# Reordering the start of the second layer of a two-layer diffusion block: weight splits, root and first norm tile interleaved, and one modulation block moved

## The reference

```python
for l in range(DEPTH):                       # DEPTH = 2
    mod = silu(c) @ ada_w[l] + ada_b[l]      # 6 * 1024 columns: shifts, scales, gates; same for c_ctx
    h = rmsnorm(x, norm_mix_pre[l]) * (1 + mod[1]) + mod[0]
    z = h @ w_in[l]                          # 1024 -> 3072: short conv, two attentions, RWKV-7
    ya, yb, yc, yd = mixers(z)
    m = sum(sigmoid(h @ w_gate[l] + b_gate[l])[i] * (y[i] @ w_branch[l][i]) for i in range(4)) @ w_o[l]
    x = x + mod[2] * rmsnorm(m, norm_mix_post[l])
    h = rmsnorm(x, norm_ffn_pre[l]) * (1 + mod[4]) + mod[3]
    u = dwconv3(h @ ffn_up[l]); x = x + mod[5] * rmsnorm((u[:2816] * silu(u[2816:])) @ ffn_down[l], norm_ffn_post[l])
```

## Time and profile before

| | us |
|---|---|
| median of 3 runs | 1652.36 (1651.51 to 1654.15) |
| profiled execution, its own time | 1652.26 |
| its span | 1650.2 |
| TensorE busy | 1586.6 (96% of the span) |
| VectorE busy | 944.0 (57%) |
| ScalarE busy | 799.6 (48%) |
| GpSimd busy | 312.5 (19%) |

### The profile page before, as it was taken

How to read it: one execution, slowest core, us unless ns; L and a number is a source line. 1 busy time by engine, 2 the same in 40 slices (tenths; PEclk the granted TensorE clock), 3 DMA queues, 4 the chain that set the end, 5 groups by cost and what they waited for, 6 DMA issues and landing times.

```text
span 1650.2 us, 33271 instructions
## 1 busy us (share of the span) xinstructions
PE 1586.6 (96%) x14140; PEld 1321.7 (80%) x14140; DVE 944.0 (57%) x1497; ACT 799.6 (48%) x1315; POOL 312.5 (19%) x251
## 2 busy tenths in 40 slices
PE   8999999988899999999999999999998889999998
PEld 6788767767678887888888886987877779899987
DVE  5364555565465569655554225655776277677764
ACT  4322456473354266443443225525766365566653
POOL 0160234323110000112222000312352220012210
PEclk9999999999999999999999999999999899999999
DMA  9753334223852352322226343843413285645453
GB/s 332 198 166 102 102 103 160 75 99 102 266 192 91 113 191 77 102 91 88 95 71 111 106 123 126 261 128 115 143 56 130 55 281 179 215 165 181 164 189 134
DMA packets 213889, 234.42 MB, mean 142 GB/s; under 512 B 5936, under 2 KB 194736, under 8 KB 213744
## 3 DMA queue, kind: packets, MB, share of 16 engines
q1 hardware_dynamic: 194208, 191.14, 35.3%
q0 software_dynamic: 14928, 34.87, 7.9%
q10 hardware_dynamic: 4608, 6.29, 1.1%
HBM read 216.55 MB, written 15.73 MB: 141 GB/s over the span
## 4 chain that ended last, share of the span: by engine, by line
PE 70%; DVE 4%; issue 3%; ACT 3%; DMA 0%; POOL 0%; ACTq 0%; DVEq 0%; POOLq 0%
PE ps L2337 15%; PE ps L2338 15%; PE ps L2339 15%; PE ps L2633 1%; PE ps L2645 1%; PE ps L2428 1%; PE ps L2794 1%; PE ps L2793 1%; PE ps L2792 1%; PE ps L2685 1%; PE ps L2402 1%; PE ps L2404 1%; PE ps L2403 1%; PE ps L2362 1%; PE ps L2363 1%
## 5 line engine op out<-in xcount | busy, mean ns | idle before, releaser
L1065 ACT ACTIVATE whi<-ring 128x1024 fp32r<-128x1024 f32 (+1 forms) x262 | 274.5, 1052 | 481.6 <-PE ps L2339 424.6
L1610 DVE TENSOR_TENSOR wlo<-ring,whi 128x1024 fp32r<-128x1024 f32 (+1 forms) x262 | 327.5, 1254 | 175.5 <-ACT whi L1065 174.8
L2337 PE MATMUL ps<-H,whi 128*128 128x256 f32 (+1 forms) x640 | 215.4, 337 | 1.8 <-DVE wlo L1610 1.8
L2339 PE MATMUL ps<-H,wlo 128*128 128x256 f32 (+1 forms) x640 | 214.9, 336 | 0.0
L2338 PE MATMUL ps<-H,whi 128*128 128x256 f32 (+1 forms) x640 | 214.9, 336 | 0.0
L2337 PE MATMUL ps<-HR,whi 128*128 128x512 f32 (+1 forms) x568 | 202.1, 356 | 0.5 <-DVE wlo L1610 0.3
L2339 PE MATMUL ps<-HR,wlo 128*128 128x512 f32 (+1 forms) x568 | 198.3, 349 | 0.0
L2338 PE MATMUL ps<-HR,whi 128*128 128x512 f32 (+1 forms) x568 | 198.2, 349 | 0.0
L2337 PEld LDWEIGHTS ps<-H,whi 128*128 128x128 f32 x640 | 122.3, 191 | 14.2 <-issue 1.9
L2338 PEld LDWEIGHTS ps<-H,whi 128*128 128x128 f32 x640 | 122.2, 191 | 12.2
L2339 PEld LDWEIGHTS ps<-H,wlo 128*128 128x128 f32 x640 | 122.3, 191 | 12.0
(11 more groups left out here) (397 smaller groups left out, 3279.9 us busy)
## 6 DMA issues: line engine op xcount, KB each, us to landing
ring<-in_ffn_up SPq DMA_DIRECT2D x44, 1024.0 KB, 5.0
ring<-in_w_gate SPq DMA_DIRECT2D x32, 1024.0 KB, 5.9
ring<-in_ada_w SPq DMA_DIRECT2D x32, 1024.0 KB, 5.3
ring<-in_w_in SPq DMA_DIRECT2D x24, 1024.0 KB, 7.6
ring<-in_ffn_down SPq DMA_DIRECT2D x10, 1024.0 KB, 5.0
ring<-in_ffn_down SPq DMA_DIRECT2D x18, 512.0 KB, 3.8
ada<-in_ada_w SPq DMA_DIRECT2D x8, 1024.0 KB, 11.7
WB<-in_w_branch POOLq DMA_DIRECT2D x8, 1024.0 KB, 6.5
```

The costliest lines, as they stand in the source:

```text
L1065: act.activation(whi[HALF_SLOT[m]][:, 0:kn, :], ring_half(raw, half, kn), ACT.Copy).then_inc(hi_done, 1)
L1610: dve.tensor_tensor(wlo[HALF_SLOT[m]][:, 0:kn, :], ring_half(raw, half, kn), whi[HALF_SLOT[m]][:, 0:kn, :].bitcast(F32), ALU.subtract).the ...
L2337: pe.matmul(o[:, c0:c1], hi[:, i, :], part(0, k), start=(k == 0), stop=False)
L2339: last = pe.matmul(o[:, c0:c1], lo[:, i, :], part(0, k), start=False, stop=(k == kn - 1))
```

## The change

Between the layers ScalarE now splits one half, makes the root, splits the second half, copies the modulation row, then does tile 0 wholly (modulate, high), splits the third half, and goes on with tile 1. VectorE follows: low part of the first half, tile 0, second half, tile 1, low 0, third half, tile 2, tile 3, low 1, and so on. The four constants are made after the norm. `norm_finish` and `norm_apply` serve the norm ahead of layer 1's feed-forward part too, where tile 0 is likewise completed first, without splits. `project_first` waits for the split halves one by one, behind the idle matmuls. These are 9 (from 11) ahead of the z tiles and 2 (from 3) ahead of the up tiles of layer 1. Of the modulation blocks of layer 1, one more is made in attention (step 10) and one fewer in ("gap", 1, 2); all blocks after the second one move on by one place in the plan.

```diff
-IDLE = {"z": 11, "up": 3}
+IDLE = {"z": 9, "up": (3, 2)}
...
-    after = [("gap", 1, 0), ("att", 1, 4)] + chunks(1) + [("gap", 1, 1)] * 2 + [("gap", 1, 2)] * 2
+    after = [("gap", 1, 0), ("att", 1, 4), ("att", 1, 10)] + chunks(1) + [("gap", 1, 1)] * 2 + [("gap", 1, 2)]
...
                 if name == ("up", l, 1, 0) and l not in FUSED:
-                    for g in (4 * l + 2, 4 * l + 3):
-                        sp.wait_ge(mm_done, done_at(("mod",) + MOD_GAP[g - 2]))
-                        ada_gap(g)
+                    sp.wait_ge(mm_done, done_at(("mod",) + MOD_GAP[4 * l]))
+                    ada_gap(4 * l + 2)
...
-            def norm_finish(l, k, src, dst):
+            def norm_finish(l, k, src, dst, splits=0):
...
-                for i in range(KT + 1):
-                    if i < KT:
-                        act.wait_ge(h_half, 8 * no + i + 1)
-                        for s in ss:
-                            v = src[:, i, 256 * s:256 * s + 256]
-                            ins = act.activation(v, v, ACT.Identity, bias=mod[:, l, shift + i, s:s + 1],
-                                                 scale=amod[:, k, i, s:s + 1])
-                        ins.then_inc(h_full, 1)
-                    if i:
-
-                        act.wait_ge(h_full, 8 * (no - 1) + i)
-                        act.activation(dst[:, 0, i - 1, c0:c1], src[:, i - 1, c0:c1], ACT.Copy).then_inc(h_hi, 1)
+                def modulated(i):
+                    act.wait_ge(h_half, 8 * no + i + 1)
...
+                def high(i):
+                    act.wait_ge(h_full, 8 * (no - 1) + i + 1)
+                    act.activation(dst[:, 0, i, c0:c1], src[:, i, c0:c1], ACT.Copy).then_inc(h_hi, 1)
+
+                for i in range(KT):
+                    modulated(i)
+                    if i != 1:
+                        high(max(0, i - 1))
+                    if i == 0:
+                        split_until(splits)
+                high(KT - 1)
...
                 if l:
-                    split_until(half_no(("z", l, Z_ORDER[0])) + SPLIT)
+                    first_z = half_no(("z", l, Z_ORDER[0]))
+                    split_until(first_z + 1)
                     norm_root(l, 0)
+                    split_until(first_z + 2)
                     fill(("gap", l, 0))
-                    norm_finish(l, 0, Z, HR)
+                    norm_finish(l, 0, Z, HR, first_z + SPLIT)
...
-            def norm_apply(l, k, src, tmp, dst):
+            def norm_apply(l, k, src, tmp, dst, splits=None):
...
                 for i in range(KT):
                     over_rms(l, k, src, tmp, i)
-                    if i >= 2:
-                        low(i - 2)
+                    if i != 2 and i:
+                        low(max(0, i - 2))
+                    if splits and i in splits:
+                        split_until(splits[i])
...
                 if l:
                     gains(l, (0,))
+                    first_z = half_no(("z", l, Z_ORDER[0]))
+                    split_until(first_z + 1)
+                    norm_apply(l, 0, X, Z, HR, {0: first_z + 2, 1: first_z + SPLIT})
+                    fill(("gap", l, 0))
...
-                if l:
-                    split_until(half_no(("z", l, Z_ORDER[0])) + SPLIT)
-                    norm_apply(l, 0, X, Z, HR)
-                    fill(("gap", l, 0))
...
                 tiles = []
-                for name in names:
-                    tiles += halves(name)
                 for _ in range(idle):
...
                 for k, n in order:
                     c0, c1 = cs[n]
+                    if n == len(tiles):
+                        tiles += halves(names[n])
...
-                              IDLE["up"])
+                              IDLE["up"][l])
```

More of the change, by code:

```diff
@@ L1087, in norm_finish @@
                 c0, c1 = cols(l) if k else (0, T)
-                for i in range(KT + 1):
-                    if i < KT:
-                        act.wait_ge(h_half, 8 * no + i + 1)
-                        for s in ss:
-                            v = src[:, i, 256 * s:256 * s + 256]
-                            ins = act.activation(v, v, ACT.Identity, bias=mod[:, l, shift + i, s:s + 1],
-                                                 scale=amod[:, k, i, s:s + 1])
-                        ins.then_inc(h_full, 1)
-                    if i:
-                        act.wait_ge(h_full, 8 * (no - 1) + i)
-                        act.activation(dst[:, 0, i - 1, c0:c1], src[:, i - 1, c0:c1], ACT.Copy).then_inc(h_hi, 1)
+                def modulated(i):
+                    act.wait_ge(h_half, 8 * no + i + 1)
+                    for s in ss:
+                        v = src[:, i, 256 * s:256 * s + 256]
+                        ins = act.activation(v, v, ACT.Identity, bias=mod[:, l, shift + i, s:s + 1],
+                                             scale=amod[:, k, i, s:s + 1])
+                    ins.then_inc(h_full, 1)
+                def high(i):
[8 more added lines that the diff above has]
+                high(KT - 1)
             act.wait_ge(c_in, 16)
```

## The result

The changed kernel takes 1659.48 us (median of 22 executions), the kernel before 1651.53 in the same comparison: ratio 1.0042, 95% interval 1.0028 to 1.0056. It is slower, by twice what a measurement can tell from no change, and outside the forecast's range.

The account below looks back on a forecast made before the run. TensorE, busy 96% of the span, was taken as the bound, with ScalarE pacing the stretch between the layers. The terms +0.1 + 0.4 - 1.0 = -0.5 us gave 1651.8 us from 1652.36; the range was 1650.0 to 1653.5.

Parts of the forecast that it names:

- Between the layers: Stretch between layers 0 and 1 in the new order: exit at 1039.18 against 1039.06, +0.1 us, bounds -0.5 and +0.6.
- norm: Norm ahead of layer 1's feed-forward part: one modulation row fewer ahead of the tiles, -1.0 us, bounds -0.7 and -1.7.
- ScalarE as the pacemaker: Between the layers ScalarE sets the chain, 1.51 us a tile, so from tile 1 on everything is 0.63 us later.
- the third split ahead of tile 2: Between the layers VectorE makes the third low part before tile 2, so ScalarE idles about 1.0 us.
- the cover at the end of attention: TensorE's waits of 1.90 us there cover the moved block's 1.54; only ScalarE's 0.38 us row copy is exposed.
- the row rate of TensorE behind row 0: In the norm ahead of layer 1's feed-forward part, TensorE at 1.08 us a row is slower than tiles at 0.87.
- One block moved into attention: Modulation block made at step 10 of layer 1's attention: +0.4 us, bounds 0 and 1.54.
- Queues: Part of the attention step: SyncE's extra ring load costs nothing; two more jobs shift later ones and keep their distances.
- What is late next: Behind the feed-forward norm: the split behind the first output tile, TensorE waiting 1.77 us, moves along as before.
- The clock: Half-clock stretches cost 1.7 us where TensorE is the bound; nothing in the sum, as 1.6 is covered between the layers.
- The stretch that I feared: Half clock invited by TensorE's idle 3.1 us ahead of row 1 between the layers; 1.7 us more without cover.
- The rival of a clock that falls for long: 10.2 us at half clock, as seen between 1304.5 and 1314.7, behind row 0 between the layers: 1655.3 us, chance 0.05.

Follow-up runs that it names:

- p_block77: The kernel before with only the modulation block moved, plus 77 waits on reached semaphores in layer 0's up projection: 1653.32 us, ratio 0.9998.
- p_before28: The kernel before plus 28 waits on reached semaphores on TensorE in layer 0's up projection: 1655.83 us, ratio 1.003.
- a_wb_first: The changed kernel, with SyncE's load of gate weights (1, 1, 3) waiting until the first load of WB has landed: 1655.29 us, ratio 1.0017.
- again_all: The changed kernel run once more, unchanged: 1658.50 us, ratio 1.0041 against the kernel before.
- p_after228: The changed kernel plus 228 waits on reached semaphores in layer 0's up projection: 1653.31 us, ratio 1.0013 against the kernel before.
- p_after256: The changed kernel plus 256 such waits in layer 0's up projection, the instructions of one 16 KB fetch: 1658.44 us, ratio 1.0046.
- e_block: The kernel before with only the modulation block moved into attention (plan and SyncE's loads): 1653.20 us, ratio 1.0007.
- p_before117: The kernel before plus 117 waits on reached semaphores in layer 0's up projection: 1653.39 us, ratio 1.0016.
- p_after89: The changed kernel plus 89 waits on reached semaphores in layer 0's up projection: 1650.90 us, ratio 1.0005 against the kernel before.
- ctrl_same: The kernel before, unchanged, timed against itself: 1651.79 us, ratio 1.0000.
- e_order: The changed kernel with the modulation blocks left in their old places (new order, idle counts and lazy wait only): 1649.99 us, ratio 0.9992.
- p_block216: The kernel before with only the modulation block moved, plus 216 waits on reached semaphores in layer 0's up projection: 1650.67 us, ratio 0.9999.

## Why the prediction was wrong

- **Between the layers, attention, norm: right.** They came to +0.20, +0.32 and -0.98 against +0.1, +0.4 and -1.0, each with the mechanism named (ScalarE as the pacemaker, the third split ahead of tile 2, the cover at the end of attention, the row rate of TensorE behind row 0). That tile 0 comes early bought nothing at the exit, as worked out.
- **"One block moved into attention": the step that failed.** Under "Queues" it has the ring load at nothing and the job numbers at nothing, and both are (p_block77 has both, and its gates stage is the 75.7 of the kernel before). What it leaves out is that the block is also 42 instructions in TensorE's stream, and that everything between attention and the norm, 250 us with the fast small matmuls of the scan, moves against the 16 KB cuts. The new order has 11 instructions fewer up to there, which makes 31, and p_before28 shows that 28 alone cost 1.003 (1.001 to 1.005) or 3.6 to 4.0 us at equal clock. It was neither a term of the sum nor a rival.
- **"What is late next" was not asked of the last product of the scan.** A stop of 1.8 us there is worth only 1.3 us by itself (from the first state product of the step to the first gate matmul 4.62 us, before 3.31, because 1.00 of waiting for YB was there already). But GpSimd's load of WB hangs on that product, and its lead over SyncE's load of the same size was 1.71 us. When the lead is gone, WB takes 3.4 us longer to land and TensorE waits 3.56 instead of 1.57. a_wb_first keeps the stop and gives a part of it back (2.4 us by the levels, 1.0 by the stage).
- **"The clock": nothing for it in the sum, and 3 to 4 us of the loss.** The changed kernel is 4.1 us slower at equal clock (1655.95 against 1651.8 to 1652.2); the rest of what lies between the means (1658.7 against 1650.9 to 1651.2 in its sets of 35) goes with a mean clock of 0.9873 in place of 0.9905 to 0.9913. The stretch that I feared, behind row 0 between the layers, came only in some profiles (none in that of after, one at 1025.6 in again_all). Others stand in the gates stage. An early one, up to 2.2 us behind the first gate matmul, is in five profiles (after, again_all, a_wb_first, p_after228, p_after256), each behind a stop of 0.9 us or more; but p_before28 has a stop of 1.21 us and no early one. A later one, 9.7 to 12.5 us behind it, is in nine: these five, e_block, p_before28, p_before117 and p_after89, where TensorE stood waiting for WL just ahead of it or inside it. In p_after89 and p_after228 that wait was no longer than in the kernel before. The five profiles with neither are before, ctrl_same, e_order, p_block216 and p_block77. From the first state product of the last step to the first w_o product the kernel before takes 79.0 us, the kernel after 84.5, p_after228, with the same 6.8 us of half clock but WB in time, 83.0, and p_before28, with half of that at half clock and WB late, 83.5: the clock and the late WB are both in the 5.5 us. The page of the Trainium skill that I cited, "TensorE: Matmul & The Clock Gate" (its part on the HAM clock gate), says that activity releases the throttle; the early stretches agree in kind, each beginning 0.4 to 2.1 us behind the end of a stop, and the idle time ahead of them was not that of the filler taken out. How the clock's share divides between the stop, the late WB and chance, these runs don't settle.
- **The rival of a clock that falls for long** took the 10.2 us of the earlier trace rows as a thing of its own. In the trace of before, a stop with the cause issue ends right inside that stretch, and the scan of layer 0 has a longer one (timeline of TensorE, kernel before):

```profile
446.80 0.27 PE L2762 MATMUL ps<-LM,nu 64*64 64x64 f32 x2 [2.79 <-issue]
```

It stands in the same kind of place, the last products of a scan. By the count above the instruction behind it has the number 10177, again 193 modulo 256, 2.29 us behind the start of a transfer. Read in time, this row and the queue of instructions would have given the rival that came true.

The Trainium skill has a section on this, "Instruction fetch mechanics" of "Runtime: NRT & Kernel Launch": the instruction memory is refilled in blocks of 16 KiB, 256 instructions, and the cost of crossing a boundary is "mostly hidden". The trace agrees on the size (113 transfers, 1.85 MB), and p_after256 and the table of stops on the count. On "mostly hidden" the measurement decides: in the stretch that runs 208 instructions in 2.50 us, the crossing cost up to 1.8 us at the stop itself, and about 4 us with what hung on it.

## What to carry to other kernels

Moving instructions on an engine moves all that stands between the old and the new place against the 16 KB cuts of its stream. Look for the stretches where small instructions run fastest, see whether the profile has a stop with the cause "issue" there or near it, and give such a stop a term or a rival. The cause "issue" alone doesn't make it a fetch: of the 13 such stops of 0.4 us or more in the two scans of the kernel before, ten stand at number 193 modulo 256, and three (1.48, 0.82 and 1.28 us) don't; these three are in the kernel after too, at the same work and as long. A few instructions added where the engine is busy with long ones put the cut elsewhere. And where two large loads on two queues go out within 2 us of each other, work out which one is needed first and what holds it ahead: if it is only timing, a wait that fixes the order takes a part of the harm out of a change elsewhere. When a change's own terms are as small as half a microsecond, look for a gap of 4 us in the stages that the diff doesn't touch too, with a table by stage.

## What the hardware showed that I had not expected

- The ten stops at a cut in the two scans of the kernel before of 0.4 us or more add up to 14.5 us; the twelve of the kernel after, with the one of 1.79, to 11.5. The changed kernel doesn't stop longer in all: what counts is what hangs on the place. What all of them together cost was not tested.
- 28 instructions that do nothing cost 0.3%, 256 of them cost 0.05% or nothing beside the same kernel without (1.0046 against 1.0041 and 1.0042), and 89 gain 0.36% in the changed kernel.
- From the start of the transfer of instructions to TensorE's next matmul it took 2.28 us in the profile after (1337.94 to 1340.22), of which the transfer itself is 0.92, while the ring's loads kept the DMA engines busy. In p_after228 it was about 2.4 (1332.47 to 1334.88).
- Two loads of 1 MB that overlap don't share evenly in their effect: the one issued up to 0.3 us behind, or less than 0.8 ahead, took 8.8 to 9.9 us to land in place of the 6.3 to 6.7 that it takes with a lead of 1.0 to 1.7.
